# The first conditioning piece ahead of x in a one-core diffusion step on Trainium2

## What is computed

```python
sh1, sc1, g1, sh2, sc2, g2 = split(silu(c) @ w_ada[l] + b_ada[l], 6)   # c or c_ctx
y  = x * rsqrt(mean(x * x) + EPS) * norm1_g[l]                         # RMSNorm
h  = y * (1 + sc1) + sh1                                               # modulate
... = h @ w_in[l]          # heads, z, xbc and dt; then attention, SSD, w_out, MoE
```

## Time and profile before

| what | value |
|---|---|
| median of 3 runs | 779.58 us (778.82 to 781.81) |
| profiled execution | 780.95 us, its span 779.2 us |
| TensorE busy | 741.1 us, 95% of the span |
| DVE, ACT busy | 582.9 us, 502.6 us |
| read from HBM | 182.79 MB |

### The profile page before, as it was taken

How to read it: one execution, slowest core, us unless ns; L and a number is a source line. 1 busy time by engine, 2 the same in 40 slices (tenths; PEclk the granted TensorE clock), 3 DMA queues, 4 the chain that set the end, 5 groups by cost and what they waited for, 6 DMA issues and landing times.

```text
span 779.2 us, 10976 instructions
## 1 busy us (share of the span) xinstructions
PE 741.1 (95%) x4020; PEld 575.5 (74%) x4020; DVE 582.9 (75%) x968; ACT 502.6 (65%) x834; POOL 50.4 (6%) x36
## 2 busy tenths in 40 slices
PE   4999999899999999999999999989999999999995
PEld 2557877458966888888779788845798788888874
DVE  3258376987566789999868746878766789999965
ACT  3049694484457777778746678457556887777852
POOL 0001342000000000000000135200000000000000
PEclk9999999999999999999999999999999999999998
DMA  9963034977338899999855113096741199999902
GB/s 364 423 249 109 7 128 143 423 272 298 109 119 364 283 380 369 375 370 362 306 212 213 61 49 103 33 378 211 291 148 54 55 329 377 378 359 378 373 21 85
DMA packets 33484, 186.20 MB, mean 239 GB/s; under 512 B 5136, under 2 KB 6288, under 8 KB 16400
## 3 DMA queue, kind: packets, MB, share of 16 engines
q1 hardware_dynamic: 33424, 185.42, 62.9%
HBM read 182.79 MB, written 2.62 MB: 238 GB/s over the span
## 4 chain that ended last, share of the span: by engine, by line
PE 77%; DVE 10%; ACT 7%; issue 4%; DMA 2%; DVEq 0%; ACTq 0%; SPq 0%
PE psum L886 23%; PE psum L915 11%; PE psum L1037 11%; PE psum L1239 5%; PE psum L1004 4%; PE psum L716 3%; PE psum L938 3%; PE psum L864 2%; DVE att L2290 1%; PE psum L767 1%; PE psum L752 1%; PE psum L1209 1%; PE psum L1107 1%; ACT split L1439 1%; DMA ring<-in_w_ada 1%
## 5 line engine op out<-in xcount | busy, mean ns | idle before, releaser
L2079 DVE TENSOR_TENSOR split<-ring,split 128x2048 fp32r<-128x2048 f32 x96 | 219.9, 2290 | 28.1 <-ACT split L1564 26.5
L1564 ACT CAST split<-ring 128x2048 fp32r<-128x2048 f32 x96 | 183.6, 1912 | 23.5 <-PE psum L915 14.4
L886 PE MATMUL psum<-split,y_hi 128*128 128x512 f32 x512 | 162.1, 398 | 0.4 <-ACT selT L1537 0.4
L886 PEld LDWEIGHTS psum<-split,y_hi 128*128 128x128 f32 x512 | 94.4, 189 | 18.9 <-issue 0.4
L886 PE MATMUL psum<-split,y_lo 128*128 128x512 f32 x256 | 100.6, 393 | 0.0
L1037 PE MATMUL psum<-ring_r,hT_hi 128*128 128x512 f32 x216 | 73.2, 393 | 0.0
L915 PE MATMUL psum<-split,hidT 128*128 128x512 f32 x256 | 69.6, 394 | 1.8 <-DVE hidT_lo L2084 1.8
L915 PEld LDWEIGHTS psum<-split,hidT 128*128 128x128 f32 x256 | 47.3, 188 | 14.1 <-DVE hidT_lo L2084 4.6
L886 PEld LDWEIGHTS psum<-split,y_lo 128*128 128x128 f32 x256 | 48.5, 189 | 10.3
L2527 POOL TENSOR_TENSOR ud<-const,da_hi 128x1024 fp32r<-128x1024 f32 x12 | 27.3, 2292 | 396.8 <-DVE da_lo L2180 389.3
L1037 PEld LDWEIGHTS psum<-ring_r,hT_hi 128*128 128x128 f32 x216 | 40.0, 188 | 8.9 <-issue 0.8
(11 more groups left out here) (314 smaller groups left out, 1427.9 us busy)
## 6 DMA issues: line engine op xcount, KB each, us to landing
ring<-in_w_gu SPq DMA_DIRECT2D x64, 1024.0 KB, 5.1
ring<-in_w_ada SPq DMA_DIRECT2D x40, 1024.0 KB, 7.0
ring<-in_w_down SPq DMA_DIRECT2D x32, 1024.0 KB, 5.1
ring<-in_w_rows SPq DMA_DIRECT2D x12, 1024.0 KB, 4.8
ring<-in_first SPq DMA_DIRECT2D x8, 1024.0 KB, 14.6
ring<-in_w_out SPq DMA_DIRECT2D x8, 1024.0 KB, 5.5
ring<-in_w_xbc SPq DMA_DIRECT2D x8, 800.0 KB, 9.2
par<-in_par SPq DMA_DIRECT2D x1, 1728.0 KB, 13.2
```

The lines of the kernel that those rows point to most:

```text
L886: last = pe.matmul(dst, x[:, g, t, :], w[:, j, :], start=(t == 0 and i == 0), stop=(t == KD - 1 and i == 2))
L1564: act.copy(splits[unit_split(n)][:, 0, :], slot(key)).then_inc(raised("whi", l, p), 1)
L2079: tt(lo, slot(unit_key(l, p, n)), hi.bitcast(F32), ALU.subtract).then_inc(raised("wlo", l, p), 1)
```

## The change: another order of the first 20 us

The new constant `FIRST_FOLD` is 2. SP fetches conditioning piece 0 right behind `pcol`, and only then x, now in four quarters with a semaphore each. ACT copies the rows of piece 0 before it squares anything. DVE folds chunks 3 to 7 onto chunk 2, and makes `mods` and `amul` of chunk 0 ahead of the scaling. TensorE begins with `first(0)`; it then multiplies ones with chunks 0 and 1 as they are squared, and with the folded chunk last. `first(1)` no longer stands ahead of the projection but behind its second product, and `first_turn(1)` and `first(2)` stand two products and one product later in chunk 0; from chunk 1 on the order is as before. Number and shape of the products stay what they were, except that DMAs of x are four instead of two.

```diff
 # SyncE
-            for half in range(2):
-                sp.dma_start(xT[:, 4 * half:4 * half + 4, :], ...).then_inc(x_in[half], 16)
...
+                if n == 1:
+                    for two in range(KD // 2):
+                        sp.dma_start(xT[:, 2 * two:2 * two + 2, :], ...).then_inc(x_in[two], 16)
 # TensorE
-            pe.wait_ge(setup_dve, 1)
-            sums(0, 0)
             pe.wait_ge(siluc_ready, 1)
...
             first(0)
+            pe.wait_ge(setup_dve, 1)
+            pe.wait_ge(*fill(("ss", 0, 0), None))
+            for c in range(FIRST_FOLD):
+                pe.wait_ge(sig["sq"], c + 1)
+                pe.matmul(bank(("ss", 0, 0))[:, 0:TOK], ones, sq[:, c, :], start=(c == 0), stop=False)
+            pe.wait_ge(sig["fold"], 1)
+            pe.matmul(bank(("ss", 0, 0))[:, 0:TOK], ones, sq[:, FIRST_FOLD, :], start=False, stop=True)\
+                .then_inc(*filled(("ss", 0, 0)))
             first_turn(0)
-            first(1)
...
-                                    if l == 0 and c == 1 and k + 1 < KD:
+                                    if l == 0 and k == 0 and c == 1:
+                                        first(1)
+                                    if l == 0 and c == (1 if k else 3) and k + 1 < KD:
                                         first_turn(k + 1)
-                                    if l == 0 and c == 4 and k + 2 < KD:
+                                    if l == 0 and c == (4 if k else 5) and k + 2 < KD:
                                         first(k + 2)
 # ScalarE: first(0) ahead of squares(0, 0); squares wait for x_in[c // 2]
 # VectorE: folds 3..7 onto 2; first(0) at the head of norm
```

More of the change, by code:

```diff
@@ L49 @@
 H_AT = 2
+FIRST_FOLD = 2
 ROUNDED = (1,)
@@ L529, in build @@
         const_in, pcol_in, par_in = (sem(n) for n in ("const_in", "pcol_in", "par_in"))
-        x_in = [sem(f"x_in{half}") for half in range(2)]
+        x_in = [sem(f"x_in{two}") for two in range(KD // 2)]
         dve_step, act_step, pool_step = (sem(n) for n in ("dve_step", "act_step", "pool_step"))
@@ L1332, in _ @@
             sp.dma_start(pcol, a["pcol"]).then_inc(pcol_in, 16)
-            for half in range(2):
-                sp.dma_start(xT[:, 4 * half:4 * half + 4, :], a["xT"][:, 4 * half:4 * half + 4, :]).then_inc(x_in[half], 16)
             def load(key):
@@ L1369, in _ @@
             for n, key in enumerate(pieces):
+                if n == 1:
+                    for two in range(KD // 2):
+                        sp.dma_start(xT[:, 2 * two:2 * two + 2, :], a["xT"][:, 2 * two:2 * two + 2, :]).then_inc(x_in[two], 16)
                 if n == 3:
@@ L1439, in out_hi, with first @@
                 act.copy(splits[out_split(n)][:, 0, :], slot(("wout", l, n))).then_inc(sig["mhi"], 1)
+            def first(j):
+                key = ("first", 0, j)
+                act.wait_ge(*full(key))
+                act.copy(ada_rows[:, 0:2 * P], bank(key)[:, 0:2 * P]).then_inc(*was_read(key))
             def split_win(l, p):
@@ L1475, in squares @@
                     else:
-                        act.wait_ge(x_in[c // 4], 16)
+                        act.wait_ge(x_in[c // 2], 16)
                     act.activation(sq[:, c, :], xT[:, c, :], ACT.Square).then_inc(sig["sq"], 1)
@@ L1592, in _ @@
                         elif not l:
+                            first(0)
                             squares(0, 0)
@@ L1600, in _ @@
                         if not (l or arg[0]):
[L1601 to L1604, removed]
+                            for j in range(1, KD):
+                                first(j)
                                 if j == KD - 2:
@@ L1869, in fold @@
                     dve.wait_ge(dve_step, dve_steps())
-            for c in range(1, KD - 2):
-                fold(c, sig["sq"], 0)
+            for c in range(FIRST_FOLD + 1, KD):
+                dve.wait_ge(sig["sq"], c + 1)
+                ins = tt(sq[:, FIRST_FOLD, :], sq[:, FIRST_FOLD, :], sq[:, c, :], ALU.add)
+                if c == KD - 1:
+                    ins.then_inc(sig["fold"], 1)
+                else:
+                    ins.then_inc(dve_step, 1)
+                    dve.wait_ge(dve_step, dve_steps())
             def first(j):
@@ L1889, in norm @@
                 key = ("ss", l, n)
+                if l == 0:
+                    first(0)
                 if l in ROUNDED:
@@ L1940, in norm @@
                     for c in range(c0, c1):
-                        first(c)
+                        if c:
+                            first(c)
                         for j, part in ((0, slice(0, P)), (1, slice(P, TOK))):
```

## The result

The changed kernel takes 781.79 us (median of 22 executions, 780.78 to 783.75), the kernel before 779.29 (22 executions). The ratio is 1.0031, interval 1.0021 to 1.0040: about 2.4 us slower (2.5 by the medians), clear of noise, though only 0.3% of the time.

A forecast was written before the change was run, and what follows sets the result against it. TensorE was taken as the bound, busy 95% of the span. Later dense work (+0.4 us) and the clock (+2.0) made +2.4 on the median 779.58, so 782.0 us, range 779.2 to 784.0.

The forecast's parts named there:

- the order: At the start, the reordered chain up to dense TensorE work: begins at 17.8 instead of 17.40, +0.4 us.
- Transfers: Loads at the start: piece 0 lands at 6.6 us, the last quarter of x at 10.4, 2.6 us late.
- slow quarters: Rival, x loads: four 384 KB pieces at the lower rate take 6.9 instead of 3.7 us; 785.2 us, chance 0.08.
- Squares, folds, sums, norm: Start chain: squares end at 12.3 us, folds at 13.5, sum at 15.25; 2.55 us later dense work begins.
- Piece 1: Moving piece 1 into the projection: no cost of its own, same work, hand-overs covered.
- The clock: TensorE's split start leaves the first dense work at the lower level: 2.0 us lost, bounds 0 to 2.7.
- The other reading: TensorE's start: only the first 5 us of work are slow whenever they come; sum about −0.3 us.
- A level that is high in time: Rival, TensorE's start: early products raise the level before 13.6 us, dense work begins at 17.1; 779.3 us, chance 0.14.
- The delay was not swallowed later: Rival, later stages: one waits for something that does not move with TensorE, so time stays at 779.6 us; chance 0.06.

The follow-up runs named there:

- the run with 9 and 5 filling products: Kernel before with sums split and x first, plus 9 filling products ahead of the sums and 5 ahead of the folded product: 779.61 us, ratio 0.9998.

## Why the prediction was right, step by step

The time came out, 781.79 against 782.0, and so did the mechanism: the order costs next to nothing, and the clock makes the change slower. Single terms did not all come out, and that the number is met to 0.2 us is luck: the start lost 3.1 us and not 2.4, and the medians show 2.5 of them.

*Transfers.* Piece 0 was there at 5.97, the last quarter of x near 10.1 (issued at 3.37, 6.7 us to landing), against 6.6 and 10.4. So the 1.57 MB of x came within 4.1 us behind piece 0, near the 3.7 of the full rate and far from the 6.9 of slow quarters; that rival is refuted:

```profile
ring<-in_first SPq DMA_DIRECT2D x1, 1024.0 KB, 4.8
...
xT<-in_xT SPq DMA_DIRECT2D x1, 384.0 KB, 6.7
```

*Squares, folds, sums, norm.* Squares from 8.3, folds to 13.05, one product of 1.66 us at the low level, projection at 17.51: each 0.3 to 0.5 us sooner than worked out, by the earlier landing. Part of it was lost on piece 0, which took 1.97 us and not 1.68: that figure came from the execution before, where the level rose at 15.43, within the piece. The order costs 0.1 and not 0.4.

*Piece 1.* Its hand-overs were covered: TensorE has no gap from 17.51 on. Having called its move free was wrong, though. It could have run in the 2.1 us in which TensorE waited for chunk 0; the run with it back ahead is 2.0 us faster than the change (1.4 by the ratios).

*The clock.* The right mechanism, undersized. I took 2.0 us, with 2.7 as the upper bound from the longest low stretch that the trace showed. Measured: rows come 3.09 later, of which 0.11 is the later beginning, so the clock cost 2.98, for 6 us at the low level (17.5 to 23.5). The bound was not one: a low stretch in another order need not be shorter than those in the trace at hand. The other reading that the prediction weighed, that only the first 5 us of work are slow, failed: by 17.51 TensorE had worked for 7.1 us in the change, and the low level went on. The Trainium skill's rule ("TensorE: Matmul & The Clock Gate", part 1, the HAM clock gate), that gaps bring the throttled level back, agrees in kind with the runs, though the gaps ahead of these falls were shorter than those that the page warns of: with 18 products filled in, the level fell at 10.19 after 2.1 us of waiting, and in the run with the copy moved it fell at 13.88, where the longest wait since the rise had been 1.47 us.

*Rivals.* A level that is high in time did not happen in the change. The delay was not swallowed later: of 3.1 us at the row projection 2.5 are in the medians. The 0.6 that are missing go the way of the later falls, of which the median execution of before has one and that of the change none.

What stays open: how long the start of an execution that was not profiled ran at the low level, since the mean clock does not count it, and why the change has fewer later falls.

## What to carry to other kernels

Work that runs while TensorE is slow need not become cheap by moving it into an idle place: in the change, and in the run with the sums split alone, the low level stayed with the first stretch of unbroken work, and whatever then came first paid. Before taking products off the chain at a start, look at what will run in the first microseconds of dense work, and at the gaps ahead of it. Here it was worth more to give TensorE something to do while it waits for the first transfer (777.45) than to reorder its work (779.14, 781.79). Fewer such products, which ended 0.5 us sooner, gave 778.77; whether that difference is more than scatter is not shown.

## What had not been expected

- The length of a gap alone did not tell whether the level would fall. It fell at 10.19 behind a wait of 2.10 us, at 15.40 behind one of 2.03, and at 13.88 with no wait longer than 1.47 since the rise; it stayed high over a wait of 1.94 us that ended at 10.16 in the run with 9 and 5 filling products, and over 0.6 and 0.4 us around 16 us in the kernel before.
- A fall lasted 3.4 or 6.8 us, and one profiled execution has two of them (before, at 254 and 524 us), another none while TensorE works (the change). The parts behind the row projection take 716.8 and 714.2 us. A pair of profiles can hide a change of 2 to 3 us; the mean clock of many executions shows it.
- The clock column shows 1.00 until the first change of level that is recorded. The low level at the start has to be read from the length of equal records, 2.90 against 1.53 us here.
